# Block 1's attention projected first, the delta rule's tiles projected between its units, and the modulation in 96 pieces

## The reference

```python
# block 1
proj = rms_norm(x) @ w_in            # qkv_dn 1536, z 512, b/a 8, qkv_att 1536, gate 512 columns
qkv_dn = silu(causal_conv4(qkv_dn)); q, k = l2_norm(q), l2_norm(k)      # 4 heads of 128
y_dn  = rms_norm(gated_delta_rule(q, k, v, g, beta)) * silu(z)
q_a, k_a = rms_norm per head of 64                                      # 8 heads
y_att = softmax attention of three dilated patterns, relative bias, * silu(gate)
x = x + concat(y_dn, y_att) @ w_out
# block 2
mod = silu(c) @ w_ada + b_ada        # 1024 x 6144: shift, scale, gate, twice
h = rms_norm(x) * (1 + scale1) + shift1; proj = h @ w_in_2
sliding-window attention with sinks, differential attention, gated merge, @ w_out_2
x = x + gate1 * ...;  h2 = rms_norm(x) * (1 + scale2) + shift2
x = x + gate2 * conv_ffn(h2);  out = rms_norm(x)
```

## Time and profile before

| what | value |
|---|---|
| median of 3 runs | 1319.36 us (1319.03 to 1320.11) |
| the profiled execution's own time | 1324.16 us |
| its span, first to last instruction | 1322.0 us |
| busy: PE, weight loads, DVE, ACT, POOL | 1177.6, 921.8, 615.9, 517.0, 508.2 us |
| mean granted TensorE clock | 0.947 of full speed |
| moved by DMA | 116.35 MB, mean 88 GB/s |

### The profile page before, as it was taken

How to read it: one execution, slowest core, us unless ns; L and a number is a source line. 1 busy time by engine, 2 the same in 40 slices (tenths; PEclk the granted TensorE clock), 3 DMA queues, 4 the chain that set the end, 5 groups by cost and what they waited for, 6 DMA issues and landing times.

```text
span 1322.0 us, 15503 instructions
## 1 busy us (share of the span) xinstructions
PE 1177.6 (89%) x5617; PEld 921.8 (70%) x5617; DVE 615.9 (47%) x1143; ACT 517.0 (39%) x844; POOL 508.2 (38%) x428
## 2 busy tenths in 40 slices
PE   6997857888878978799999998999799999989997
PEld 5675635555557966576777776787588888878886
DVE  3678265667565632235554667531643333330002
ACT  5467334333353333354443445441633333321114
POOL 5434423233260123433334324154354444443443
PEclk9899968888888998999999999899899999989999
DMA  8654755454210001222222221223133333332211
GB/s 165 156 120 112 170 148 147 124 175 160 79 32 1 1 1 45 63 64 93 67 64 64 64 64 65 64 96 84 44 95 96 96 98 99 102 102 74 95 63 64
DMA packets 107405, 116.35 MB, mean 88 GB/s; under 512 B 4065, under 2 KB 96439, under 8 KB 107348
## 3 DMA queue, kind: packets, MB, share of 16 engines
q1 hardware_dynamic: 98800, 86.58, 24.5%
q0 software_dynamic: 8160, 28.05, 6.5%
q10 hardware_dynamic: 388, 0.96, 0.2%
HBM read 113.46 MB, written 2.12 MB: 87 GB/s over the span
## 4 chain that ended last, share of the span: by engine, by line
PE 72%; DVE 9%; DMA 7%; ACT 5%; POOL 3%; issue 2%; SPq 0%; DVEq 0%; ACTq 0%
PE bank L654 19%; PE bank L655 19%; PE bank L656 19%; DMA ada_w<-w_ada 5%; POOL wlo L444 3%; PE bank L808 3%; DMA raw<-w_in 2%; PE bank L918 2%; PE bank L833 2%; PE bank L816 2%; PE bank L929 1%; ACT whi L1151 1%; DVE conv L1574 1%; DVE ryy L1477 1%; PE bank L689 1%
## 5 line engine op out<-in xcount | busy, mean ns | idle before, releaser
L444 POOL TENSOR_TENSOR wlo<-raw,whi 128x512 fp32r<-128x512 f32 x312 | 419.2, 1373 | 530.0 <-ACT whi L1151 529.9
L654 PE MATMUL bank<-h_hi,whi 128*128 128x512 f32 x1016 | 419.8, 413 | 32.3 <-DVE h_lo L1467 17.6
L655 PE MATMUL bank<-h_lo,whi 128*128 128x512 f32 x1016 | 403.1, 397 | 0.0
L656 PE MATMUL bank<-h_hi,wlo 128*128 128x512 f32 x1016 | 402.7, 396 | 0.0
L654 PEld LDWEIGHTS bank<-h_hi,whi 128*128 128x128 f32 x1016 | 195.6, 193 | 101.6 <-issue 42.0
L1151 ACT ACTIVATE whi<-raw 128x2048 fp32r<-128x2048 f32 (+1 forms) x79 | 150.1, 1900 | 191.9 <-PE bank L656 178.4
L656 PEld LDWEIGHTS bank<-h_hi,wlo 128*128 128x128 f32 x1016 | 195.0, 192 | 43.2
L655 PEld LDWEIGHTS bank<-h_lo,whi 128*128 128x128 f32 x1016 | 195.7, 193 | 40.5 <-issue 3.3
L1263 ACT ACTIVATE pT_a<-bank 128x256 f32<-128x256 f32 (+3 forms) x80 | 32.5, 406 | 202.1 <-PE bank L816 202.1
L1558 DVE SCALAR_TENSOR_TENSOR ada_acc<-ada_w,small,ada_acc 128x1024 f32<-128x1024 f32 x42 | 61.4, 1463 | 64.9 <-DMA ada_w<-w_ada 64.2
L654 PE MATMUL bank<-ffn_hi,whi 128*128 (+1 forms) x176 | 70.9, 403 | 4.1 <-DVE ffn_lo L1467 4.1
(11 more groups left out here) (310 smaller groups left out, 1539.2 us busy)
## 6 DMA issues: line engine op xcount, KB each, us to landing
raw<-w_in SPq DMA_DIRECT2D x66, 512.0 KB, 5.8
ada_w<-w_ada POOLq DMA_DIRECT2D x48, 512.0 KB, 4.9
raw<-w_up SPq DMA_DIRECT2D x44, 512.0 KB, 4.6
raw<-w_down SPq DMA_DIRECT2D x22, 512.0 KB, 4.1
raw<-w_out SPq DMA_DIRECT2D x16, 512.0 KB, 5.1
x_tok<-x SPq DMA_DIRECT2D x4, 512.0 KB, 5.5
toe<-bias_rows POOLq DMA_DIRECT2D x8, 256.0 KB, 5.5
raw<-w_branch_swa SPq DMA_DIRECT2D x4, 512.0 KB, 3.5
```

The costliest lines, as they stand in the source:

```text
L444: ins = pool.tensor_tensor(wlo[s][:, c], raw[s][:, c], whi[s][:, c].bitcast(F32), ALU.subtract)
L654: pe.matmul(ps, wh, h_hi, start=start, stop=False)
L655: pe.matmul(ps, wh, h_lo, start=False, stop=False)
L656: return pe.matmul(ps, wl, h_hi, start=False, stop=stop)
```

## The change

- **Stage 0** has 7 blocks: block 0, then the attention's q, k (tiles 1 to 8) and values (9 to 12), with the attention's 8 norms.
- **a1** has four steps a unit instead of two, after 8 steps ahead of the first unit: 16 tiles, 12 of them the delta rule's. For these ACT writes the first tap (a scaled copy), DVE the other three (L1574's form), without the Silu.
- **After a1**: three Silus over four tiles each, the 8 norms of q and k with squares on POOL and four sets of buffers, and between PE's sums the last 32 steps (4 gate tiles), evacuated by DVE.
- **The modulation** comes in 96 pieces of 128 rows by 512 columns (256 KB), loaded by ACT: 16 in stage 0, 32 in a1 (one a unit), 8 in the delta rule's levels, 8 in S1, 32 in a2. ACT's load for unit w + 1 stands after its tail of unit w. 12 folds of four products with one column each write the columns of bank 7 directly; DVE adds b_ada (now a part of colB) at the next fold. The selector matrix, the row buffers and the turning after a1 go; the second scale is prepared after a2.
- **a2** writes all its outputs in one bank (bank 6), since bank 7 now collects the modulation, and so waits before each new output for the copy of the one before, as a1 does.

```diff
-        ADA_STEP = {n: 1 for n in range(1, 7)} | {n: 3 for n in range(7, 12)}
-        ADA_S0 = sum(ADA_STEP.values())
-
-        OFFS = [2048] + [256 * n for n in range(6)] + [2056 + 256 * n for n in range(6)] + [1536, 1792] \
+
+
+
+
+        ADA_S0 = {T: (T - 1, T) if T <= 8 else (2 * T - 10, 2 * T - 8) for T in range(1, 13)}
+        ADA_A1, ADA_DN, ADA_S1, ADA_A2, ADA_N = 16, 48, 56, 64, 96
+
+        OFFS = [2048] + [2056 + 256 * n for n in range(6)] + [256 * n for n in range(6)] + [1536, 1792] \
             + [2056 + 256 * n for n in (6, 7)]
-        S0_BLOCKS = 13
+        S0_BLOCKS = 7
...
+            for n in range(S0_BLOCKS + 1, N_S1):
+                lo(n)
+
+            pool.wait_ge(S["dn_silu"], 2)
+            for j, k in enumerate(DN_TILES):
+                if j >= 4:
+                    pool.wait_ge(S["sum_done"], 8 + j - 3)
+                pool.tensor_tensor(nsq4[j % 4][:, :], qkv[:, k, :], qkv[:, k, :], ALU.mult).then_inc(S["sq_done"], 1)
+            lo(N_S1)
...
-        QK, TB, OB = (2, 3), (4, 5), {"a1": (6, 6), "a2": (6, 7), "a3": (6, 7)}
+        QK, TB, OB = (2, 3), (4, 5), {"a1": (6, 6), "a2": (6, 6), "a3": (6, 7)}
...
-        dil_steps = lambda w: min(2 * (w + 1), 4 * 2 * KT)
+        dil_steps = lambda w: min(8 + 4 * (w + 1), 128)
+        norm_steps = lambda w: 128 + 4 * (w + 1)
         swa_steps = lambda w: min(4 * (w + 1), 128)
         diff_steps = lambda w: min(136 + 6 * (w + 1), 28 * KT)
 
 
-        FILL = {dil_steps: (S0_BLOCKS, 25, 0, 32, 0), swa_steps: (FILL_N, FILL_T, 0, 32, 0),
+        FILL = {dil_steps: (S0_BLOCKS, 13, -1, 32, 0), norm_steps: (S0_BLOCKS, 13, 0, 8, 128),
+                swa_steps: (FILL_N, FILL_T, 0, 32, 0),
                 diff_steps: (FILL_N, FILL_T, -1, 16, 128)}
...
-            def fold(c):
-
-                pe.wait_ge(S["ada_piece"], 8 * (c + 1))
-                for j in range(8):
-                    jj = 8 * c + j
-                    mm = pe.matmul(bank[7][0:48, 0:P], select[:, 47 - jj:95 - jj], ada_acc[c % 2][:, j * P:(j + 1) * P],
-                                   start=jj == 0, stop=jj == 47)
+            def fold(f):
+
+                pe.wait_ge(S["ada_piece"], 8 * (f + 1))
+                for j in range(4):
+                    mm = pe.matmul(bank[7][:, 4 * f + j:4 * f + j + 1], ada_acc[:, j * P:(j + 1) * P], m(C_ONE)[:, 0:1],
+                                   start=True, stop=True)
                 mm.then_inc(S["ada_fold"], 1)
-
 
             for n in range(S0_BLOCKS):
                 if n == 0:
 
                     pe.wait_ge(S["rms_lo"], before("n0", "lo") + 1)
-                gemm(n, tiles_of(n)[0], (0,) if n == 0 else (0, 1), ready=(S["rms_lo"], before("n0", "lo") + 1) if n == 0 else None)
+                if n == 5:
+                    gemm(n, tiles_of(n)[0], (0,))
+                    fold(0)
+                    gemm(n, tiles_of(n)[1], (1,))
...
+            fold(1)
+            gate_steps(dil_steps, -1)
...
-                for c in range(ADA_S0 // 8, 6):
-                    if w == 8 * (c + 1) - ADA_S0 + 1:
-                        fold(c)
+                unit_fold(ADA_A1, w)
+
+            def unit_fold(p0, w):
+                if 8 <= w <= 32 and w % 8 == 0:
+                    fold(p0 // 8 + w // 8 - 1)
...
-            pe.wait_ge(S["modrow_ready"], 1)
-            pe.transpose(bank[4][:, 0:48], modrow[:, :], ident[0:48, 0:48]).then_inc(S["mod_tr"], 1)
-
+            def head_sum(j):
+                pe.wait_ge(S["sq_done"], 8 + j + 1)
+                if j >= 4:
+                    pe.wait_ge(S["nt_done"], 8 + j - 3)
+                pe.matmul(bank[2 + j % 4][:, :], m(C_ONE), nsq4[j % 4][:, :], start=True, stop=True).then_inc(S["sum_done"], 1)
+
+            for w in range(8):
+                gate_steps(norm_steps, w)
+                if w >= 1:
+                    head_sum(w - 1)
+            head_sum(7)
 
             pe.wait_ge(S["g_ready"], 1)
             pe.wait_ge(S["in_masks"], 16)
             for T in range(29, 33):
                 evac(pe, T)
+            pe.wait_ge(S["nt_done"], 16)
...
+                    pe.wait_ge(S["norm_done"], 16)
+                    pe.wait_ge(S["mod_add"], 6)
...
+            loaded = [0]
+
+            def ada_loads(n):
+
+                while loaded[0] < min(n, ADA_N):
+                    p = loaded[0]
+                    f, kt = divmod(p, KT)
+                    if p >= 2:
+                        act.wait_ge(S["ada_piece"], p - 1)
+                    act.dma_start(ada_w[p % 2][:, :], a["w_ada_2"][0, kt * P:(kt + 1) * P, f * SEQ:(f + 1) * SEQ])\
+                        .then_inc(S[f"ada_in{p % 2}"], 16)
+                    loaded[0] += 1
...
+                    if tag != "a3" and w < len(units):
+                        ada_loads((ADA_A1 if tag == "a1" else ADA_A2) + w + 2)
...
+                    if steps is dil_steps and t < 12:
+                        act.wait_ge(S["tile_ready"], T + 1)
+                        act.activation(dst, gate_bank(T)[:, :], ACT.Copy, scale=col("conv_w", 36 + t)).then_inc(S["conv_tap"], 1)
+                    elif t % 2 == 0:
                         act.wait_ge(S["tile_ready"], T + 1)
                         act.activation(dst, gate_bank(T)[:, :], ACT.Copy, scale=scale).then_inc(S[f"evac{T % 4}"], 1)
-                    else:
+                    if t % 2 == 1:
                         hi(FILL[steps][0] + t // 2 + 2)
...
+            for T in range(13, 25):
+                evac(act, T)
+            for f in (4, 0, 8):
+                act.activation(qkv[:, f:f + 4, :], qkv[:, f:f + 4, :], ACT.Silu).then_inc(S["dn_silu"], 1)
+            ln_exp()
+            for j in range(8):
+                act.wait_ge(S["sum_done"], 8 + j + 1)
+                if j >= 4:
+                    act.wait_ge(S["norm_done"], 8 + j - 3)
+                rsqrt(bank[2 + j % 4][:, :], nry4[j % 4][:, :], nryy4[j % 4][:, :], "rs_done")
+                if j == 3:
+                    hi(N_S1)
...
+                    if c % 2 == 1 and l < 4:
+                        ada_loads(ADA_DN + 2 * l + c // 2 + 2)
+                if l == 0:
+                    hi(N_S1 + 1)
...
+            def mod_add(n):
+
+                while added[0] < n:
+                    f = slice(4 * added[0], 4 * added[0] + 4)
+                    dve.wait_ge(S["ada_fold"], added[0] + 1)
+                    dve.tensor_tensor(modc[:, f], bank[7][:, f], b_ada[:, f], ALU.add).then_inc(S["mod_add"], 1)
+                    added[0] += 1
...
+                    if steps is dil_steps and t < 12:
+                        dve.wait_ge(S["conv_tap"], t + 1)
+                        for k in range(1, 4):
+                            ins = dve.scalar_tensor_tensor(dst[:, k:], ps[:, 0:SEQ - k], col("conv_w", 12 * (3 - k) + t), dst[:, k:],
+                                                           op0=ALU.mult, op1=ALU.add)
+                            if k < 3:
+                                link(ins)
+                        ins.then_inc(S[f"evac{T % 4}"], 1)
...
-                if piece[0] < 48:
+                if w < 32:
...
+            mod_add(6)
+            scale_col(g1c, ROWS_A["norm1_g"], 8)
+            for j, k in enumerate(DN_TILES):
+                if j % 2 == 0:
+                    gate_tiles(norm_steps, j + 1)
+                dve.wait_ge(S["rs_done"], 8 + j + 1)
+                newton(bank[2 + j % 4][:, :], nry4[j % 4][:, :], nryy4[j % 4][:, :], ("nt_done", 8 + j + 1))
+                dve.scalar_tensor_tensor(qkv[:, k, :], qkv[:, k, :], -0.5 * P ** -0.5 if k < 4 else -0.5, nryy4[j % 4][:, :],
+                                         op0=ALU.mult, op1=ALU.mult).then_inc(S["norm_done"], 1)
...
+                    if c % 2 == 1 and l < 4:
+                        ada()
+            mod_add(ADA_DN // 8 + 1)
...
```

## The result

The changed kernel takes **1312.31 us** (median of 7 runs, 1307.97 to 1316.90); the kernel before took 1320.27 beside it. The ratio is 0.9926 (95% interval 0.9899 to 0.9954), a gain of 0.7% where 2.5% was forecast. The profiled execution took 1312.31 with a span of 1310.5, 11.5 less than the span before.

The account below looks back on a forecast made before the run. TensorE was taken to bound a2 but not stage 0 and a1, held up by waits for modulation pieces. -117.3 + 31 + 31.7 + 7 + 14 + 1.5 = -32.1 us, so 1287 from 1319.4; range 1262 to 1312.

Parts of the forecast that it names:

- Stage 0, -117.3: Up to a1's first attention score: moving six blocks out brings that score at 122.6 instead of 239.9 us.
- Of the 2.90 us wait for brow ... 96: Stage 0, before block 3: 1.5 us of this wait and about 1 at block 1 go, so block 5 ends at 96.
- copy and turning of the values are hidden behind the last piece: End of stage 0: value work adds no time, as the last modulation piece is added only at 116.3 us.
- a1, +31: First attention: 155 us against 124.2, with bounds of +3 and +60.
- the loop: a1, every pair of units: copy, tap, rounding, load, piece, taps, probabilities and turning in sequence; 5.2 to about 8.1 us without landing.
- L = 4: a1: issue and landing of a 256 KB modulation piece takes 4 us beside weights, 2.9 beside none.
- Behind a1, +31.7: Between a1 and the delta rule: eight norms, Silus and gate copies make 37.4 us instead of 5.7 (25 to 40).
- TensorE's 32 steps and eight sums are under it: Between a1 and the delta rule: TensorE's 21.8 + 7.5 us are hidden under VectorE's slower norms, 2.35 us each.
- a2, +14: Second attention: eight pairs of units take 9.2 us against 7.31, the others stay hidden; 3 to 30.
- Rival (a): Whole kernel: TensorE bounds, loads land early enough; a1 127, a2 125, total 1248 us; chance 0.2.
- (b): Mainly a1: slower landings beside w_in's weights; at 7.5 us each a1 takes some 210, total 1342; chance 0.1.
- (c): Norms after a1 cost 8 us more, a1 8 more, as wlo and squares shut VectorE out; 1303 us; chance 0.15.

Follow-up runs that it names:

- the best run: Changed kernel with third buffer, loads ahead of the turning wait, two Ln/Exp table loads in stage 0, early sums, last gate copy behind norms: 1263.96 us.

## Why the prediction was wrong

The direction held, the size did not: -8 to -11 us for -32. Step by step:

- **Stage 0, -117.3 against -101.5: wrong by 15.8, in two steps of 6.1 and 9.7.** "Of the 2.90 us wait for brow ... 96" for block 5's end: without the fold that now stands in it, it ended 5.6 us later than that (102.6 less 1.0), and in that stretch VectorE's piece at 79.23 took 5.50 us beside a wlo, with the norms behind it; without loads the same place costs the same (6.56 us, on a norm's second step), and block 6 ended at 115.4 there. The meeting is not all of it: in the best run it is there too (5.74 us), and block 5 ended at 98.25, fold included. So the cause of this first step is open in part. And "copy and turning of the values are hidden behind the last piece": block 6's steps ended at 115.85, and the turning began at 127.88. The norm of tiles 7 and 8 stands on ScalarE behind loads that wait for VectorE, and VectorE's copies of tiles 11 and 12 stand behind that norm. This second step lies within the 12 us that the run without loads takes away (138.4 to 126.4). Table loads are part of that queue, 24 before a1 in the kernel before and 12 still, one of them ahead of each norm.
- **a1, +31 against +45.2: wrong by 14.2, by two terms of the loop that were wrong in opposite directions.** The loop as such was right: VectorE waits for pieces, TensorE for probabilities, and taking the turning out of the loop takes 34.6 us away. The term that was mis-sized is L = 4 "beside weights, nearer the quiet rows because a piece is half as large". In the six long pairs it was 9.0 on average (54 us in all), which alone adds 30. Against that, "copy pT 0.5, the convolution's first tap 0.6, in every second pair the rounding 1.9" are not in the loop at all, since the load was issued ahead of them: 3.0 less in each long pair, 18 in all. From one pair's scores to the next the six took 77.9 us where I had 66; what stands behind the landing took them 4.0 each, as I had it (4.05). The ten other pairs with the ends took 91.5 where I had 89. That there were six long pairs was luck: they are long by the meeting with SP's raw transfers and not by a rounding ahead of the load. Without loads a1 takes 128.9 and not 124. I had taken L as a property of the stage, and it belongs to the moment: the load is issued within 2 us of a raw transfer's issue every time it matters. The row that said so was before me, 15.7 at most in the earlier trace rows.
- **Behind a1, +31.7 against +36.1.** "TensorE's 32 steps and eight sums are under it" was wrong: they set the pace. The norms begin at 317.7 on ScalarE, after eight steps that took 7.3 us at a mean clock of 0.75, and each takes one sum and four steps, 3.62 us, where I had 2.35. The total came near by my allowances, which was luck.
- **Delta rule and w_out, +7 against +4.9.** Right in kind: the run without loads gives 2.1 of it to the order.
- **a2, +14 against +3.2.** Wrong by 10.8 in the other direction, by the same step as in a1: of the 9.2 us of the loop, the copy's 0.5 and the rounding's 1.9 do not stand ahead of the load (it was issued at 600.84, the rounding began at 601.02). The rest, 6.8, is covered by TensorE's 7.31, with landings of 4.2 at most. Rival (a) held here. What is left is three folds of about 1 us.
- **The rivals.** (b) gave a wrong time and the right cause: landings beside w_in. I reckoned with landings of 6 and more throughout; the median stayed at 2.8 and six values decided. I gave it 0.1. (c) has the 5 to 6 us operation in stage 0, which again lasted as long as a whole wlo, against a loss of 16 that it forecast elsewhere; in a1 no meeting above 1.8 us stands in the chain.
- **The rule against it** held in what it says: ScalarE's pieces of half the size land beside weights in up to 13.7 us, GpSimd's took up to 15.7. My answer, that the order in the queue is worth more, held only for a queue position that the change did not take; it put the load behind TensorE's turning instead of behind 6.92 us of wlo.
- **The sum itself.** I priced the change as one thing. The runs without loads say that the new order is worth 5.4 us, and that each kernel loses 55 to 57 us to the modulation's loads; that was the larger prize. Single edits took 30 (early load), 43 (third buffer) and 33 to 38 (row spacing, with other weights) of it in the changed kernel and 14 in the kernel before. Two sums in the text are off by 1 us and cancel: 66 + 46 + 39 + 3 is 154, and eight pairs of 1.9 in a2 are 15.

## What to carry to other kernels

Before costing a moved load, take the loads out of both versions in thought: what is left is the reordering's worth, and what the loads cost is a separate sum with its own remedy (issue before the wait, or one more buffer). For a landing use not the median but the rows of transfers issued at the same moment; where two queues are released at the same point of a repeating pattern, as here 0.6 to 1.8 us apart, they can meet in every round. Read from the trace, and not from the order of the list, what a load waits for. A short stall of TensorE costs more than its idle time when the granted clock falls after it: here 12.7 us on top of 27.8.

## What was unexpected of the hardware

- Rows 16416 bytes apart (1 KB read of each) made 512 KB land in 8.9 to 9.4 us (median, 48 to 98 us) instead of 5.1 to 5.6, and cost the changed kernel 35 to 45 us in all; 16384, 16448, 16640 and 17408 do not. Pieces beside them landed in 13.8 at most instead of 5.2 to 6.6.
- In a1 TensorE's granted clock had a mean of 0.89 with the stalls and 0.99 without, its two levels being 1.2 and 2.4 GHz; after the 9.2 us wait that ended at 196.4 the first three products of a step, from 198.62 on, took 0.79, 0.63 and 0.63 us in place of 0.40.
- A load that stands behind a copy, a tap and a rounding in ScalarE's list was issued 0.09 us after the copy began, ahead of the other two (168.88 against 169.18 and 169.75).
